# One joined table of expert rows, 64 tokens x 2 picks per gather, and a dot-to-sum chain for every gather

## What is computed

```python
def block_fn(xb):                                   # 128 tokens
    q = (xb @ wq).reshape(128, 8, 2, 128)
    s = einsum('thcd,chkd->thck', q, keys)
    sv, si = top_k(s, 16)
    cand = sv[:, :, 0, :, None] + sv[:, :, 1, None, :]
    top, sel = top_k(cand.reshape(128, 8, 256), 16)
    eidx = take_along_axis(cidx, sel)               # 128 picks per token
    gate = softmax(top)
    act = gelu(einsum('td,thkd->thk', xb, u_tab[eidx]))
    return einsum('thk,thkd->td', gate * act, v_tab[eidx])
```

## Time and profile before

| | us |
|---|---|
| median of 3 runs | 1912.31 |
| lowest, highest | 1903.66, 1913.88 |
| span of the profiled execution, first to last instruction | 1891.7 |
| PE busy in it | 1079.0 |
| DVE busy | 978.1 |
| POOL busy | 998.2 |
| ACT busy | 192.3 |
| bytes moved by DMA | 685.11 MB, mean 362 GB/s |

### The profile page before, as it was taken

One profiled execution on the slowest core, in us unless ns is written; L12 is line 12 of the kernel. 1 busy time (PEld: TensorE's weight loads), 2 busy tenths in 40 slices (PEclk: granted clock), 3 DMA queues, 4 the chain that ended last, 5 costly groups with the idle time before them and its releaser, 6 DMA issues. The chain is left out here.

```text
span 1891.7 us, 17959 instructions
## 1 busy us (share of the span) xinstructions
PE 1079.0 (57%) x6318; PEld 499.7 (26%) x6318; DVE 978.1 (52%) x2585; ACT 192.3 (10%) x332; POOL 998.2 (53%) x1062
## 2 busy tenths in 40 slices
PE   8840257788955835385655874048885522045556
PEld 4420133433412422241112432024341211031113
DVE  1498975523445788954004576951344497850001
ACT  3200021201101200000000212000110000000002
POOL 0156534345465555656666353755446566656663
PEclk9965668789987967697676886578896765576678
DMA  8699869889999999989999799979999999999995
GB/s 333 244 359 379 337 244 410 337 359 399 357 360 406 423 410 421 404 343 419 371 366 386 256 421 365 408 286 418 368 337 366 402 374 381 396 330 372 368 367 206
DMA packets 172759, 685.11 MB, mean 362 GB/s; under 512 B 19616, under 2 KB 21344, under 8 KB 158190
## 3 DMA queue, kind: packets, MB, share of 16 engines
q0 software_dynamic: 152064, 553.72, 75.9%
q1 hardware_dynamic: 20606, 130.25, 17.3%
HBM read 677.66 MB, written 6.59 MB: 362 GB/s over the span
## 5 line engine op out<-in xcount | busy, mean ns | idle before, releaser
L2105 DVE SCALAR_TENSOR_TENSOR rows<-rows,acc 128x1024 f32<-128x1024 f32 x512 | 594.2, 1217 | 49.6 <-issue 26.7
L908 PE MATMUL bank<-wring,turned 128*128 128x512 f32 (+1 forms) x808 | 394.0, 635 | 40.6 <-DMA wring<-in_w 24.3
L1235 PE MATMUL acc<-rows,wz 128*32 128x512 f32 x1952 | 323.1, 783 | 143.6 <-DMA rows<-in_v,index_tb 102.6
L1450 POOL DMA_INDIRECT rows<-in_u,index_A x256 | 240.3, 939 | 303.2 <-DVE rows L2105 123.8
L1450 POOL DMA_INDIRECT rows<-in_v,index_ta x256 | 242.5, 947 | 234.1 <-PE acc L1235 142.2
L1450 POOL DMA_INDIRECT rows<-in_u,index_B x256 | 240.7, 940 | 179.1 <-DVE rows L2105 110.7
L1450 POOL DMA_INDIRECT rows<-in_v,index_tb x256 | 241.1, 942 | 138.7 <-issue 68.1
L908 PEld LDWEIGHTS bank<-wring,turned 128*128 128x128 f32 x808 | 160.5, 207 | 236.7 <-issue 205.7
L1235 PEld LDWEIGHTS acc<-rows,wz 128*32 128x32 f32 x1952 | 69.6, 130 | 351.9 <-issue 347.0
L1185 PE MATMUL bank<-xn_s,consts 128*128 128x128 f32 x256 | 48.6, 334 | 154.3 <-issue 154.3
L1185 PEld LDWEIGHTS bank<-xn_s,consts 128*128 128x128 f32 x256 | 42.9, 243 | 159.9 <-issue 159.9
(11 more groups left out here) (320 smaller groups left out, 1054.4 us busy)
## 6 DMA issues: line engine op xcount, KB each, us to landing
wring<-in_w SPq DMA_DIRECT2D x103, 1024.0 KB
out_sample<-scratch SPq DMA_DIRECT2D x2, 2128.5 KB
scratch<-in_c_s SPq DMA_DIRECT2D x2, 2064.0 KB
rows<-in_u,index_A POOLq DMA_INDIRECT x256
rows<-in_v,index_ta POOLq DMA_INDIRECT x256
rows<-in_u,index_B POOLq DMA_INDIRECT x256
rows<-in_v,index_tb POOLq DMA_INDIRECT x256
kept<-in_w SPq DMA_DIRECT2D x2, 1024.0 KB
```

The lines of the kernel that those rows point to most:

```text
L908: ins = pe.matmul(ps[:, part], turned["A"][:, 4 * h + c, :], w[:, c, part], start=first, stop=end, skip_group_check=True)
L1235: ins = pe.matmul(acc[i * QUAD:(i + 1) * QUAD, c, :], wz[:, i, at:at + QUAD], row, start=first, stop=end, skip_group_check=True)
L1450: pool.indirect_dma_start(out=rows[:, n % RING, :], out_offset=None, in_=a[table], in_offset=bass.IndirectOffsetOnAxis(ap=which[:, at:at + ...
L2105: dve.scalar_tensor_tensor(u, u, 1.0, acc[:, :, :], ALU.mult, ALU.mult, accum_out=dots[kind][:, s:s + 1]).then_inc(u_used, 1)
```

## The change

`u` and `v` are joined on the host in one table `uv` with rows of 8 KB. A gather brings 128 rows of 8 KB: 64 tokens x 2 picks for A and B, 8 tokens x 16 picks for S. There are 528 gathers of 1 MB, in a ring of 7 slots with as many bytes as before. A prompt tile is done in two parts of 64 tokens, each with 64 gathers.

For each gather there is now a chain: DVE takes the dots from the `u` half (128 at once, against `shown` in PSUM, which PE fills for each part); ACT applies gelu to a column of 128, multiplies it with the share, and multiplies a constant `fold` with it into `weighted` (128 x 64); PE multiplies `weighted` with the `v` half into the two strips of 64 partitions of `acc`. The slot is freed by that product. The indices and the shares are brought to the new layout by PE (`turn_index`, `turn_prob`) for each batch of heads, as soon as they are chosen, and the first gather waits for `turn_index`. At a part's end ACT copies `acc`, PE moves it to its place and DVE adds it to `x` (`place`). `LATE` is dropped, the PSUM banks go from 6 to 5, and the planner's numbers are set anew.

```diff
-RING = 14
-GROUP = 4
+RING = 7
+STATS = 8
-BANKS = 6
+BANKS = 5
...
-        rows = sb("rows", P, RING, D)
+        rows = sb("rows", P, RING, 2 * D)
...
+            def by_token(name, src, t, h0, h1):
+                ps = opened(name, t, h0)
+                n = PER_HEAD * (h1 - h0)
+                for part in range(2):
+                    for s in range(2):
+                        ins = pe.matmul(ps[s * 64:(s + 1) * 64, part * n:(part + 1) * n], const("ident")[:, part * 64:(part + 1) * 64],
+                                        by_slot(src, h0, h1, s), start=True, stop=True)
+                closed(ins, name, t, h0)
...
+            def vals(t, part, i):
...
+                    for c in range(2):
+                        ins = pe.matmul(acc[c * 64:(c + 1) * 64, :], weighted[:, n % STATS, :], row[:, c * BLOCK:(c + 1) * BLOCK],
+                                        start=first, stop=end, skip_group_check=True)
+                ins.then_inc(v_used, 1)
...
+            for n, (t, part, i) in enumerate(GATHERS):
...
+                    pool.wait_ge(v_used, n - RING + 1)
                 pool.indirect_dma_start(
-                    out=rows[:, n % RING, :], out_offset=None, in_=a[table],
-                    in_offset=bass.IndirectOffsetOnAxis(ap=which[:, at:at + 1], axis=0),
+                    out=rows[:, n % RING, :], out_offset=None, in_=a["uv"],
+                    in_offset=bass.IndirectOffsetOnAxis(ap=index[kind][:, part, i:i + 1], axis=0),
                 ).then_inc(row_in[n % RING], 16)
...
+            def dots_weights(t, part, i):
...
+                act.wait_ge(u_used, n + 1)
+                after(act.activation(of_row, of_row, ACT.Gelu_apprx_tanh))
...
+                after(act.activation(of_row, of_row, ACT.Copy, scale=share[kind][:, part, i:i + 1]))
+                if n >= STATS:
+                    act.wait_ge(v_used, n - STATS + 1)
...
+                    ins = act.activation(weighted[:, n % STATS, :], const("fold"), ACT.Copy, scale=of_row)
+                ins.then_inc(weights_ready, 1)
...
+            def take_dots(t, part, i):
...
+                dve.wait_ge(row_in[n % RING], 16 * (n // RING + 1))
+                u = rows[:, n % RING, 0:D].rearrange("p (c n) -> p c n", c=2)
+                dve.scalar_tensor_tensor(u, u, 1.0, shown[:, :, :], ALU.mult, ALU.mult,
+                                         accum_out=dots[kind][:, part, i:i + 1]).then_inc(u_used, 1)
...
-        "u": f["peer_u"].reshape(DEPTH * EXPERTS, D),
-        "v": f["peer_v"].reshape(DEPTH * EXPERTS, D),
+        "uv": np.concatenate([f["peer_u"], f["peer_v"]], axis=2).reshape(DEPTH * EXPERTS, 2 * D),
```

More of the change, by code:

```diff
@@ L340 @@
     "sources": (("DVE", 0.2),), "pairs": (("PE", 0.5), ("DVE", 2.2)), "choose": (("DVE", 1.2),),
-    "turn_s": (("PE", 0.4), ("DVE", 0.4)), "weights": (),
-    "turn3": (("PE", 0.4), ("ACT", 0.4)), "gate": (("PE", 1.0), ("ACT", 0.3)), "add": (("DVE", 0.4),),
-    "dots": (("PE", 1.8 * DOTS), ("DVE", 0.6)), "vals": (("PE", 1.8),)}
+    "turn_s": (("PE", 0.4), ("DVE", 0.4)),
+    "turn3": (("PE", 0.4), ("ACT", 0.4)), "gate": (("PE", 1.0), ("ACT", 0.3)), "place": (("DVE", 0.4),),
+    "vals": (("PE", 0.5),)}
 NEEDS = {
@@ L414, in first @@
             ready = max(ready, self.done["state", t - 1])
-        if stage == "show" and t:
-            ready = max(ready, self.done["add", t - 1])
         if stage in ("project", "mix", "query", "gate", "embed") and not is_kept(e):
@@ L494, in tile_of, with opens @@
     return PASS_TILES[e[1]][-1] if e[0] == "embed" else e[1]
-def turning(groups):
-    return sum(e[0] == "dots" for e in groups) <= DEC // DOTS + HOLD and any(KIND[e[1]] == "S" for e in groups)
+OPENS = {"turn": 2, "turn2": 2, "turn3": 2, "gates": 1, "cum": 1, "spread": 1, "turn_qk": 2, "scores": 1, "turn_prod": 1, "values": 4,
+         "state_args": 1, "state": 2, "sample_args": 1, "sample_read": 2, "sample_write": 2, "heads": 1, "pool_r": 1, "pool": 1,
+         "turn_pq": 1, "match": 1, "lists": 1, "pairs": 1, "turn_index": 1, "turn_prob": 1, "turn_s": 1, "place": 2, "embed": 4, "norm": 1}
+def opens(e):
+    return 1 - e[3] if e[0] in ("project", "mix", "query", "gate") else OPENS.get(e[0], 0)
 def woven(groups, stages, clocks, out, beside=(), later=()):
-    groups, stages, beside, later, waited, half_done = list(groups), list(stages), list(beside), list(later), 0, set()
+    groups, stages, beside, later, waited, half_done = list(groups), list(stages), list(beside), list(later), 0, {}
     def emit(e):
@@ L530, in woven @@
             queue = ranked or beside or later
+        if queue and not fits(queue[0]):
+            queue = next(q for q in (plain, beside, later) if q and fits(q[0]))
         engines = ("PE", "DVE") if not groups else ("DVE",) if groups[0][0] == "dots" else ("PE",)
-        of_group = clocks.run(groups[0], False, engines) if groups and ready_for(groups[0], out) else None
-        waiting = not queue or queue[0][0] == "turn3" and ("add", queue[0][1]) not in out
+        of_group = clocks.run(groups[0], False, engines) if groups and fits(groups[0]) and ready_for(groups[0], out) else None
+        waiting = not queue or queue[0][0] == "turn3" and ("place", queue[0][1], PARTS[KIND[queue[0][1]]] - 1) not in out
         of_stage = None if waiting else clocks.run(queue[0], False, engines)
@@ L538, in woven @@
             take = "group" if of_stage is None else "stage"
-        elif half_done and groups[0][0] == "dots" and KIND[groups[0][1]] == "S":
-            take = "stage"
-        elif groups[0][0] in ("dots", "gelu", "weights") and turning(groups):
-            take = "group"
-        elif groups[0][0] in ("show", "gelu", "weights", "refill", "add"):
+        elif groups[0][0] in ("show", "place"):
             take = "group" if of_group[1] <= of_stage[1] + 0.5 else "stage"
@@ new lines, in place @@
+            def place(t, part):
+                if KIND[t] == "S":
+                    dve.wait_ge(v_used, last_of(t, part) + 1)
+                    after(dve.tensor_tensor(x["S"][:, :], x["S"][:, :], acc[:, 0:HALF], ALU.add), acc_read)
+                    return
+                mine = slice(part * 64, (part + 1) * 64)
+                for c in range(2):
+                    of_x = x[KIND[t]][mine, c * BLOCK:(c + 1) * BLOCK]
+                    ps = full("place", t, part, c)
+                    free(dve.tensor_tensor(of_x, of_x, ps[mine, :], ALU.add), "place", t, part, c)
@@ L2179, in _ @@
                   "sources": sources, "best": find_best, "soften": soften, "choose": choose, "embed": embed, "apply": apply,
-                  "turn_index": turn_index, "turn_s": turn_s, "dots": take_dots, "gelu": gelu, "weights": weights, "refill": refill, "add": add_experts}
+                  "turn_index": turn_index, "turn_prob": turn_prob, "turn_s": turn_s, "dots": take_dots, "place": place}
             for e in SCHEDULE:
```

487 lines of the change are left out of this document (200 added, 287 removed).

## The result

The changed kernel takes **1812.84 us** (median of 4, 1810.32 to 1817.85), the kernel before beside it 1910.24 us (1903.66 to 1913.88). The ratio is 0.947, with an interval of 0.942 to 0.952: 5.3% faster. The forecast was 1866 us, 2.4% faster. The direction and the range held; the size was missed by more than half of the gain.

What follows compares the result with a forecast made beforehand. Bytes moved by DMA were taken as the bound: start 89, dense 1138, gathers alone 384 and last stage 235 make 1846, with 20.6 around the span 1866 us, 2.4% below 1912.3; range 1785 to 1950.

Steps and rivals of the forecast that it cites:

- Gathers alone: Stages 785 to 985 and 1459 to 1655 us, gathers mostly alone: 396 us at 383 GB/s become 384 us at 395.
- last stage: The final 237 us: 7 us off for faster gathers, 5 us more for a longer tail, so 235 us.
- 20.6 us lie around the span: Difference between the 1891.7 us span and the 1912.3 us median, added to the 1846 us sum to give 1866.
- Dense stages: Gathers beside dense work, 86 to 785 and 985 to 1459 us: 368 GB/s becomes 379, 1173 us becomes 1138.
- slow rival: Held slots starve the queue in dense stages; below 364 GB/s it is slower, at 350 the time is 1962 us; chance 0.27.
- Packets: Gather transfers: packets double to 8 KB, so gathers move 3.2% faster; bounds nothing and 10%.
- my marks of 73 and 75: Queue q0's share on the page: near 73% expected; 75% or more denies the packet term.
- off the sum: ACT's 54 more table loads, 69 us (144 by the skill's figure), add no time as long as ACT has room.
- Start: Before the first gather: 86 us and 3 us more, since indices now pass through PE, a bank and a copy.
- tail: End of the last stage, after tile B's last gather: 5 us more; growth over 15 us would make the prediction wrong.
- The slower side: Whole kernel: the changed kernel comes out slower than the kernel before, the slow rival's outcome; chance 0.27.

Runs made afterwards that it cites:

- first condition: Series of runs in which the unaltered kernel before took near 1910 us, as in the result; the changed kernel's ratio there is 0.947.
- second condition: Series of runs in which the unaltered kernel before took 1733 us; the changed kernel's ratio there is 1.045.
- c1: The changed kernel itself, unaltered, run again in a series where the kernel before took 1732.8 us: 1814.4 us.
- b1: The kernel before, unaltered, run again for its trace in a series where the kernel before took 1732.6 us: 1731.3 us.
- e3: The changed kernel with POOL waiting for one sum more before each gather, so six of seven slots are used: 1859.6 us, ratio 0.969 to the kernel before.
- e6: The changed kernel with ACT copying the dots instead of taking their gelu, so no table is loaded for it: 1796.0 us.
- e5: The changed kernel without the second strip's half of the weighted sums, except for the first gather of a part: 1813.6 us.

## Why the prediction was right or wrong

**Gathers alone: the step that failed.** "151.6 MB in 396 us, 383 GB/s; with 3.2% it is 395". The changed kernel moved 169 MB alone at 427 (more than 151.6, since part of what the sum had as its last stage runs alone too). At 395 that is 428 us, and it took 396: 32 us of the miss of 53. The prediction said that POOL "can refill the ring at once after a stall" and gave it no term, having read 1.27 us a gather as the sign that POOL could hardly catch up. The sign was right and worth a term. The gaps of 3.3 us and the dip behind them stood in the trace of before and were not looked for. Between the gaps the rate was 420 already; with half as many issues the gaps could be made up for, and 420 or a little more would have been the better forecast. What could not be read there is that the gaps are absent in another series.

**"20.6 us lie around the span": a wrong reading.** In every run that lists both, the span is 1.8 to 2.3 us below the time, for either kernel (here 1808.1 and 1810.3). The 1891.7 us were those of an execution that was itself some 18 us faster than the median. The 20.6 should have been 2, and the sum, 1848, compared with 1893.8. That is 2.4% less too, so the forecast ratio stands; only its 1866 us are 18 us too long. Span against span, 46 us were forecast (1891.7 to 1846) and 84 measured (1891.7 to 1808.1).

**Dense stages: the right number, in part by luck.** Forecast 379 GB/s, measured about 380. The point from which the slow rival would have decided, 364, was cleared. That holds for the first condition only, where gaps had pressed down the 368 itself. The kernel before in the second condition shows what its dense stages do without them:

```profile
87.00:752.00 665.00, 387.89 (x2269) 195.53 (x2267) 470.83 (x1275) 87.79 (x153) 370.82 (x392) 0.76 0.98 397
926.00:1345.00 419.00, 262.24 (x2064) 127.89 (x2068) 252.83 (x680) 51.20 (x93) 249.07 (x265) 0.79 1.01 408
```

There 397 and 408 stand against 372 in 89 to 831 and 384 in 949 to 1490 in c1. The new chain loses some 6% beside dense work. The old mean of 368 was 8% low for another reason, the first condition (b1's two stretches give 401), and with the 3.2% added it came to nearly the same place: two errors that cancelled. In the second condition the slow rival is what happens. That held slots cost time there, e3 shows; that they make up the whole loss is argued, not shown.

**Packets: right.** q0's share of 74.3% lies between my marks of 73 and 75. Per MB it is 38.8 us of one engine, 6.5% below the 41.5 of before, and 2% below b1's 39.6. A single packet tells it better than the sums, which hold some long ones: q0's median packet of 4 KB takes 159 ns in before and in b1, the one of 8 KB 309 ns, 2.8% less per byte, where I had 3.2%. The rule of the Trainium skill that I set against this term (*DMA: Bandwidth & Descriptors*, section Specifications: line rate from 512 bytes up) is nearly right in the second condition, 419 GB/s with rows of 4 KB and 427 with 8 KB. Even these 8 GB/s need not be the packets', since POOL issues 4 KB rows at no more than 423 GB/s. In the first condition the rule says nothing of the 58 GB/s between 369 and 427, and some 50 of those go with the gaps in the issue.

**POOL, DVE, PE, ACT.** POOL is busy 499.7 us; an issue takes 0.94 us as before, so a larger row costs POOL nothing. DVE is at 994 us, the dots at 1220 ns each. The sums take 706.8 us, inside 510 to 960, and PE 1374, inside 1215 to 1665. The strips overlap, as these rows of the changed kernel show at the full clock, with the chain of ACT behind a dot:

```profile
1601.33 1.04 PE L1214 MATMUL acc<-rows,weighted 128*64 128x512 f32 x4
1602.82 0.20 ACT L1602 ACTIVATE dots_B<-dots_B 128x1 f32<-128x1 f32 x1 [2.44 <-DVE rows L2088]
1603.05 0.29 ACT L1607 ACTIVATE dots_B<-dots_B,share_B 128x1 f32<-128x1 f32 x1
1603.38 0.35 ACT L1613 ACTIVATE weighted<-consts,dots_B 128x64 f32<-128x64 f32 x1
```

ACT came to 695 us, not 580: it spends 0.84 us of instructions per gather where I had 0.6. The loads are as forecast, 54 more (105 for 51), 43 of them at the gelu. I had called them off the sum. e6 shows 17 us for 59 loads and the gelu, so the ring hides most of their 76 us, not all, and 17 us are 0.3 us for each load, below its own 1.28. The larger price that the Trainium skill, *ScalarE: Activation LUTs*, section What ACT_TABLE_LOAD costs, would put on them (a drain of about 1.38 us more each) cannot be seen in a row.

**Start right, tail 8 us short.** 89 us before the first gather. Behind the last issue (1768.26) lie 40 us; forecast 32 by my own rates, 23 before. The prediction also called itself wrong as a whole if the tail after tile B's last gather grew by more than 15 us. Counted from that issue, it grew from 35 us (1857.05 to 1891.7) to 65 (1743.34 to 1808.1). The sign was ill chosen: before, the last gathers of tile B were those of `LATE`, and from tile B's last addition to the end it is 57 us before and 43 now (1765.53 to 1808.1). The sum's own error here is the 8 us.

**The slower side.** The prediction gave it 0.27 and decided by the dense rate. The second condition makes it come true at 1.045. I had taken the times of before as a property of the kernel. They are one of the kernel and of a condition that the three runs of one series could not reveal. That the sign came out right was thus luck: it hung on the condition of the series.

## What to carry to other kernels

Read the issuing engine's timeline for its longest gap and the windows just behind it: an issue rate that only equals the transfer rate can make up for nothing, so that each gap is lost in full, and more bytes per issue buy the slack. A difference between a profiled span and a median is first of all the spread between executions; take the overhead from a run that lists both. And if a gain rests on a wait whose releaser had already finished by the records, measure the old kernel again in another series before trusting the sign. A forecast that meets its number for a stage can still rest on two errors that cancel.

## What was not expected of the hardware

- The same kernel had two stable times 10% apart, 1733 and 1893 to 1920 us. In the slow one POOL's waits for PE include "remote" ones (24 to 35 of them, 51 to 83 us in all) and gaps of 3 to 5 us; the fast one has none in the kernel before. PE's signals reach the trace up to several us after the work (178 of 483 by more than 0.5 us, against 8 of 532 in the second condition; the changed kernel has 33 of 897 in the first). What sets the condition was not found: the kernel's fills on POOL and the pattern of the indices do not, and the recording is a suspect that was not tried. The kernel with one gather per MB does not feel it (1813 and 1814 us). Whether it is the number of gathers, of their packets (144 each at either size) or POOL's slack that protects them was not tried apart.
- One strip of 64 columns costs PE as much time as two (720.6 and 706.8 us in all); e5 shows it.
- After a gap of 3.3 us in the issue the transfers took 11 us to come back from 217 to 417 GB/s, though issues went on every 1.24 us.
